# mLSTM stage: the old state's part is multiplied from unscaled q, scaled and added in SBUF, and the products that spread maxima and decays move behind the next turning and the k projection

## The reference

```python
mt = jnp.maximum(a, jnp.max(dmat, axis=-1))          # stabiliser of each token
w_inter = jnp.exp(a - mt)                            # weight of the old state
s = einsum('td,sd->ts', qb, kb) * jnp.exp(dmat - mt[..., None])
num = einsum('ts,sv->tv', s, vb) + w_inter[..., None] * einsum('td,dv->tv', qb, c)
den = jnp.sum(s, axis=-1) + w_inter * einsum('td,d->t', qb, n)
h = num / jnp.maximum(jnp.abs(den), jnp.exp(-mt))[..., None]
c_new = w_c * c + einsum('s,sd,sv->dv', w_s, kb, vb)
h_m = sigmoid(o) * rmsnorm(h, g_head)
```

## Time and profile before

| | |
|---|---|
| median of 3 runs | 2672.49 us (2671.37 to 2673.51) |
| the profiled execution: its time, its span | 2674.39 us, 2672.5 us |
| PE busy | 2589.0 us, 97% of the span |
| DVE busy | 1879.7 us, 70% |
| ACT busy | 906.3 us, 34% |
| chain that ended last | PE 88%, DVE 7% |
| mean granted clock of PE | 0.988 of full speed |

### The profile page before, as it was taken

One profiled execution on the slowest core, in us unless ns is written; L12 is line 12 of the kernel. 1 busy time (PEld: TensorE's weight loads), 2 busy tenths in 40 slices (PEclk: granted clock), 3 DMA queues, 4 the chain that ended last, 5 costly groups with the idle time before them and its releaser, 6 DMA issues.

```text
span 2672.5 us, 41483 instructions
## 1 busy us (share of the span) xinstructions
PE 2589.0 (97%) x14465; PEld 2239.6 (84%) x14465; DVE 1879.7 (70%) x3250; ACT 906.3 (34%) x2075; POOL 80.3 (3%) x167
## 2 busy tenths in 40 slices
PE   7999999999999998999999899999899999999998
PEld 6888888877887867999999798999778888887886
DVE  7666676764545568777777888888887887885444
ACT  4333333443333343222222333232432232342332
POOL 0000000000000000000000000000000000001010
PEclk9999999999999998999999999999999999999999
DMA  5112111442322334221111441222242222234221
GB/s 205 56 56 82 55 55 62 162 151 95 106 106 91 109 108 163 88 67 63 63 63 63 150 134 63 94 67 90 63 152 79 78 64 77 78 138 173 89 71 54
DMA packets 165561, 252.72 MB, mean 95 GB/s; under 512 B 11168, under 2 KB 114696, under 8 KB 165480
## 3 DMA queue, kind: packets, MB, share of 16 engines
q1 hardware_dynamic: 163128, 243.12, 27.4%
q0 software_dynamic: 2352, 8.52, 1.0%
HBM read 194.48 MB, written 56.95 MB: 94 GB/s over the span
## 4 chain that ended last, share of the span: by engine, by line
PE 88%; DVE 7%; issue 2%; ACT 1%; DMA 1%; POOL 0%; SPq 0%; DVEq 0%; ACTq 0%; POOLq 0%
PE m_proj L112 12%; PE m_proj L114 12%; PE m_proj L113 12%; PE m_turned L112 6%; PE m_turned L113 6%; PE m_turned L114 6%; PE m_acc L114 5%; PE m_acc L113 5%; PE m_acc L112 5%; PE m_pair L112 4%; PE m_pair L113 4%; PE m_pair L114 4%; PE m_pair L1222 1%; DVE f_acc L2142 1%; PE m_turned L1230 1%
## 5 line engine op out<-in xcount | busy, mean ns | idle before, releaser
L1916 ACT ACTIVATE f_up_hi<-f_sums 128x512 fp32r<-128x512 f32 x144 | 89.5, 622 | 544.1 <-DVE f_sums L2098 497.0
L2114 DVE TENSOR_TENSOR f_part<-f_part,m_acc 128x384 f32<-128x384 f32 (+2 forms) x240 | 119.3, 514 | 144.3 <-PE m_acc L114 142.0
L112 PE MATMUL m_proj<-f_down_hi,f_uT_hi 128*128 128x512 f32 x512 | 205.0, 400 | 8.1 <-DVE f_acc L2142 7.9
L112 PE MATMUL m_turned<-f_down_hi,f_uT_hi 128*128 128x512 f32 x512 | 201.4, 393 | 10.5 <-DVE f_down_lo L2111 10.5
L113 PE MATMUL m_turned<-f_down_lo,f_uT_hi 128*128 128x512 f32 x512 | 201.3, 393 | 0.0
L114 PE MATMUL m_turned<-f_down_hi,f_uT_lo 128*128 128x512 f32 x512 | 201.0, 393 | 0.0
L113 PE MATMUL m_proj<-f_down_lo,f_uT_hi 128*128 128x512 f32 x512 | 200.6, 392 | 0.0
L114 PE MATMUL m_proj<-f_down_hi,f_uT_lo 128*128 128x512 f32 x512 | 200.6, 392 | 0.0
L2142 DVE TENSOR_TENSOR f_acc<-f_acc,m_turned 128x1024 f32<-128x1024 f32 x143 | 166.3, 1163 | 34.3 <-PE m_turned L114 32.2
L2142 DVE TENSOR_TENSOR f_acc<-f_acc,m_proj 128x1024 f32<-128x1024 f32 x128 | 156.1, 1219 | 46.5 <-PE m_proj L114 46.5
L1932 ACT ACTIVATE f_uT_hi<-f_part 128x256 fp32r<-128x256 f32 (+1 forms) x320 | 98.3, 364 | 206.7 <-PE m_turned L114 124.8
(11 more groups left out here) (389 smaller groups left out, 7146.6 us busy)
## 6 DMA issues: line engine op xcount, KB each, us to landing
f_up_raw<-in_w_up SPq DMA_DIRECT2D x96, 512.0 KB, 5.3
f_down_raw<-in_w_down SPq DMA_DIRECT2D x96, 512.0 KB, 5.3
hT_hi_kept<-m_hT_hi SPq DMA_DIRECT2D x17, 512.0 KB, 4.9
hT_lo_kept<-m_hT_lo SPq DMA_DIRECT2D x17, 512.0 KB, 5.7
a_hT_hi<-hT_hi_kept SPq DMA_DIRECT2D x17, 512.0 KB, 3.6
a_hT_lo<-hT_lo_kept SPq DMA_DIRECT2D x17, 512.0 KB, 4.6
m_x<-in_x_prompt SPq DMA_DIRECT2D x16, 512.0 KB, 4.2
a_x_sum<-in_x_prompt SPq DMA_DIRECT2D x16, 512.0 KB, 6.4
```

What stands on the lines that cost most here:

```text
L112: eng.matmul(out, lh(k), rh(k), start=f, stop=False)
L1916: act.activation(up_hi[:, q], weight(q), ACT.Copy).then_inc(up_hi_made, 1)
L2114: dve.tensor_tensor(part[out][:, 0:w], part[other][:, 0:w], up_ps[bank][:, 0:w], ALU.add).then_inc(combined, 1)
```

## The change

It does five things.

1. q is no longer scaled (DVE L796) and no scaled q is turned (PE L672) or copied (ACT L549).
2. The old state's part is multiplied from unscaled turned q right behind the v projection, four products into `past`, a view of `turned`. DVE scales it out of PSUM with the column of w_inter into a new SBUF tile `num`.
3. `acc` holds the tokens' part alone; DVE adds it to `num` in SBUF ahead of the final part. The final part, the four squares on ACT and `heads` then read `num`. The squares wait for the sum, and the wait for the squares moves three small operations later.
4. On PE the products L637 to L641 move behind `turn_h` of the next tile and the k projection. On DVE the copies of COLS and the masking move behind `split_h` and `output_gate`; on ACT taking k moves ahead of the exponentials.
5. Waits: `turn_h` and the attention's first turning wait for `past_sb` in place of `qsT_sb`; the product into `acc` waits for `num_sb` of the tile before in place of the end of `heads`.

```diff
 # scalar(act), body
             if exists(r + 1):
                 split_h(tile_at(r + 1, 1 - slot))
+            if exists(i) and not first_round(r):
+                take_k(cur)
...
-            if exists(i) and not first_round(r):
-                take_k(cur)
...
-            if exists(j):
-                all_of(act, qs_turned, j)
-                all_of(act, squared, j - 1)
-                act.activation(qsT[:, :, 0:mix.n], turned[:, 0:HEADS, 0:mix.n], ACT.Copy).then_inc(qsT_sb, 1)
...
-                all_of(act, num_ps, j)
+                all_of(act, num_sb, j)
                 reached(act, fin_step, (j - 1) * FIN_STEPS + 10)
                 for h in range(HEADS):
-                    ins = act.activation(junk[0:mix.n, h, :], acc[0:mix.n, h, 0:QK], ACT.Square, accum_out=fin[0:mix.n, 3, h:h + 1])
+                    ins = act.activation(junk[0:mix.n, h, :], num[0:mix.n, h, 0:QK], ACT.Square, accum_out=fin[0:mix.n, 3, h:h + 1])
 # tensor(pe), body
+            if exists(r + 1):
+                turn_h(tile_at(r + 1, 1 - slot))
+            if exists(i) and not first_round(r):
+                all_of(pe, o_sb, i - 1)
+                project(proj[1], cur, w_k, k_ps)
             if exists(j):
                 all_of(pe, row_act, j, ROW_ACTS)
...
-            if exists(r + 1):
-                turn_h(tile_at(r + 1, 1 - slot))
-            if exists(i) and not first_round(r):
-                all_of(pe, o_sb, i - 1)
-                project(proj[1], cur, w_k, k_ps)
...
-                all_of(pe, q_scaled, j)
                 all_of(pe, qT_sb, j)
                 all_of(pe, kT_sb, j)
+                if m == P:
+                    all_of(pe, C_moved, j - 1)
+                state = C if m == P else C_dec
                 for h in range(HEADS):
-                    ins = pe.transpose(turned[:, h, 0:m], q[0:m, mix.slot, h * QK:(h + 1) * QK], ident[0:m, 0:m])
-                ins.then_inc(qs_turned, 1)
+                    ins = pe.matmul(past[0:m, h, :], qT[:, h, 0:m], state[:, h, :], start=True, stop=True)
+                ins.then_inc(past_ps, 1)
...
-                all_of(pe, fin_step, j - 1, FIN_STEPS)
+                all_of(pe, num_sb, j - 1)
...
                 for h in range(HEADS):
-                    pe.matmul(acc[0:m, h, 0:VA], qsT[:, h, 0:m], state[:, h, :], start=True, stop=False)
-                    ins = pe.matmul(acc[0:m, h, 0:VA], decay[0:m, h, 0:m], v[0:m, mix.slot, h, :], start=False, stop=True)
+                    ins = pe.matmul(acc[0:m, h, 0:VA], decay[0:m, h, 0:m], v[0:m, mix.slot, h, :], start=True, stop=True)
 # vector(dve), body
-            if exists(j):
-                all_of(dve, cols_ps, j)
...
             if exists(r + 1):
                 split_h(tile_at(r + 1, 1 - slot))
...
                 if exists(i):
                     output_gate(mix)
+                all_of(dve, cols_ps, j)
+                dve.tensor_copy(cols[0:m, 0:12], COLS[0:m, 0:12]).then_inc(cols_sb, 1)
+                dve.tensor_copy(cols[:, 12:16], COLS[:, 12:16]).then_inc(cols_sb, 1)
+
+                all_of(dve, num_ps, j - 1)
+                dve.scalar_tensor_tensor(decay[0:m, :, 0:m], wide[0:m, :, 0:m], -1.0,
...
-                qv = q[0:m, mix.slot, :].rearrange("p (h d) -> p h d", h=HEADS)
-                dve.tensor_tensor(qv, qv, cols[0:m, 4:8].unsqueeze(2).to_broadcast([m, HEADS, QK]), ALU.mult).then_inc(q_scaled, 1)
...
+                all_of(dve, past_ps, j)
+                all_of(dve, cols_sb, j, 2)
+                all_of(dve, fin_step, j - 1, FIN_STEPS)
+                dve.tensor_tensor(num[0:m], past[0:m], cols[0:m, 4:8].unsqueeze(2).to_broadcast([m, HEADS, VA]), ALU.mult).then_inc(past_sb, 1)
                 all_of(dve, scores_ps, j)
...
-                all_of(dve, squared, j)
-                dve.tensor_tensor(f(0), acc[0:m, :, QK], cols[0:m, 8:12], ALU.max).then_inc(fin_step, 1)
+                dve.tensor_tensor(num[0:m], num[0:m], acc[0:m, :, 0:VA], ALU.add).then_inc(num_sb, 1)
+                all_of(dve, num_sb, j)
+                dve.tensor_tensor(f(0), num[0:m, :, QK], cols[0:m, 8:12], ALU.max).then_inc(fin_step, 1)
...
                 dve.reciprocal(f(2), f(1)).then_inc(fin_step, 1)
                 dve.wait_ge(fin_step, base + 6)
+                all_of(dve, squared, j)
                 dve.tensor_tensor(f(4), f(3), f(2), ALU.mult).then_inc(fin_step, 1)
 # attention, tensor(pe)
-                pe.wait_ge(*m.qsT_sb)
+                pe.wait_ge(*m.past_sb)
```

More of the change, by code:

```diff
@@ L213 @@
     o_sb: object
-    qsT_sb: object
+    past_sb: object
     cols_sb: object
@@ L296, in mlstm_programs @@
     x, gmix = sb("x", [P, 2, D]), sb("gmix", [P, D])
+    hT_hi, hT_lo = sb("hT_hi", [P, 2, KC, P], F32R), sb("hT_lo", [P, 2, KC, P], F32R)
+    num_at = sb.next
     w_raw = sb("w_raw", [P, PC])
-    hT_hi, hT_lo = sb("hT_hi", [P, 2, KC, P], F32R), sb("hT_lo", [P, 2, KC, P], F32R)
+    num = Place(nc, "m_", num_at, IDENT_AREA)("num", [P, HEADS, VA])
     q, k = sb("q", [P, 2, MW]), sb("k", [P, 2, MW])
     v, o = sb("v", [P, 2, HEADS, VA]), sb("o", [P, 2, MW])
-    qkT, qsT = sb("qkT", [P, 2, HEADS, P]), sb("qsT", [P, HEADS, P])
+    qkT, junk = sb("qkT", [P, 2, HEADS, P]), sb("junk", [P, HEADS, P])
     qT, kT = qkT[:, 0], qkT[:, 1]
@@ L356, in mlstm_programs @@
     proj = [both[:, 0, :], both[:, 1, :]]
-    turned = ps("turned", [P, KC, P])
+    turned = ps("turned", [P, KC, P])[:]
     pair = ps("pair", [P, 2, NB])
@@ L363, in mlstm_programs @@
     first_q, first_k = (acc[:, 2 * n:2 * n + 2, :].rearrange("p a b -> p (a b)") for n in (0, 1))
-    junk = qsT
+    past = turned.rearrange("p c t -> p (c t)").rearrange("p (h v) -> p h v", h=HEADS)[:, :, 0:VA]
     ident_made, consts_in, const_sb = sem("ident_made"), sem("consts_in"), sem("const_sb")
@@ L374, in mlstm_programs @@
     cols_ps, cols_sb, masked, decayed = (sem(n) for n in ("cols_ps", "cols_sb", "masked", "decayed"))
-    qk_turned, qT_sb, kT_sb, q_scaled, k_scaled = (sem(n) for n in ("qk_turned", "qT_sb", "kT_sb", "q_scaled", "k_scaled"))
-    qs_turned, qsT_sb, scores_ps, state_ps = (sem(n) for n in ("qs_turned", "qsT_sb", "scores_ps", "state_ps"))
+    qk_turned, qT_sb, kT_sb, k_scaled = (sem(n) for n in ("qk_turned", "qT_sb", "kT_sb", "k_scaled"))
+    past_ps, past_sb, num_sb, scores_ps, state_ps = (sem(n) for n in ("past_ps", "past_sb", "num_sb", "scores_ps", "state_ps"))
     weighted, C_made, C_moved, num_ps, squared, fin_step, out_done, state_out = (
@@ L738, in heads @@
                 at = slice(h * QK, (h + 1) * QK)
-                ins = dve.scalar_tensor_tensor(heads_out[0:m, at], acc[0:m, h, 0:QK], fin[0:m, 7, h:h + 1], o[0:m, t.slot, at],
+                ins = dve.scalar_tensor_tensor(heads_out[0:m, at], num[0:m, h, 0:QK], fin[0:m, 7, h:h + 1], o[0:m, t.slot, at],
                                                ALU.mult, ALU.mult)
@@ L773, in body @@
                 yield
+            if exists(r + 1):
+                split_h(tile_at(r + 1, 1 - slot))
             if exists(j):
+                if on_round(r, 1):
+                    dve.wait_ge(late_in, 16 * N_LATE)
+                if exists(i):
+                    output_gate(mix)
                 all_of(dve, cols_ps, j)
@@ L786, in body @@
             if exists(j):
-                if on_round(r, 1):
-                    dve.wait_ge(late_in, 16 * N_LATE)
-                if exists(i):
-                    output_gate(mix)
                 all_of(dve, qk_turned, j)
                 dve.tensor_copy(kT[:, :, 0:m], turned[:, HEADS:2 * HEADS, 0:m]).then_inc(kT_sb, 1)
-                all_of(dve, cols_sb, j, 2)
-                qv = q[0:m, mix.slot, :].rearrange("p (h d) -> p h d", h=HEADS)
-                dve.tensor_tensor(qv, qv, cols[0:m, 4:8].unsqueeze(2).to_broadcast([m, HEADS, QK]), ALU.mult).then_inc(q_scaled, 1)
                 if on_round(r, NT + 1):
@@ L858, in body @@
                 f = lambda a: fin[0:m, a, :]
-                all_of(dve, squared, j)
-                dve.tensor_tensor(f(0), acc[0:m, :, QK], cols[0:m, 8:12], ALU.max).then_inc(fin_step, 1)
+                dve.tensor_tensor(num[0:m], num[0:m], acc[0:m, :, 0:VA], ALU.add).then_inc(num_sb, 1)
+                all_of(dve, num_sb, j)
+                dve.tensor_tensor(f(0), num[0:m, :, QK], cols[0:m, 8:12], ALU.max).then_inc(fin_step, 1)
                 dve.wait_ge(fin_step, base + 4)
-                dve.scalar_tensor_tensor(f(1), acc[0:m, :, QK], -1.0, f(0), ALU.mult, ALU.max).then_inc(fin_step, 1)
+                dve.scalar_tensor_tensor(f(1), num[0:m, :, QK], -1.0, f(0), ALU.mult, ALU.max).then_inc(fin_step, 1)
                 dve.wait_ge(fin_step, base + 5)
@@ L877, in mlstm_programs @@
                     q_ps=(q_ps, NT + 1), k_ps=(k_ps, NT + 1), v_ps=(v_ps, NT + 1), o_ps=(o_ps, NT + 1), v_sb=(v_sb, NT + 1), o_sb=(o_sb, NT + 1),
-                    qsT_sb=(qsT_sb, NT + 1), cols_sb=(cols_sb, 2 * (NT + 1)), weighted=(weighted, NT + 1),
```

(1 more changed line is left out.)

11 lines of the change are left out of this document (3 added, 8 removed).

## The result

The median went from 2673.0 us (4 runs) to 2697.9 us (4 runs, 2697.2 to 2698.7): ratio 1.0091, 95% interval 1.0079 to 1.0103. The change makes the kernel slower by 0.9%. The direction was forecast; the size was not: 2687 with a range to 2697. The profiled execution of after took 2697.21 us with a span of 2695.4, that is 22.9 more than the span of before.

A forecast was written before the change was run, and what follows sets the result against it. PE was taken to bound the kernel, with a lengthened DVE and ACT chain newly holding it. Profiled 2674.4 + 11.8 (rounds) - 0.9 (other rounds) + 3.4 (hand-over) = 2688.7; less 1.9 for the median, 2686.8, given as 2687, range 2676 to 2697.

The forecast's parts named there:

- What bounds the kernel: In the thirteen mLSTM rounds: PE sets the pace, busy 381.00 of 381.35 us, 29.33 us a round.
- PE's own saving: On PE in each round: four transposes go, 0.44 us, and the stall at L637 goes, 0.19 us.
- that case: At turn_gates: PE is not held, so a round takes 28.73 us and the time is 2667; chance 8%.
- The chain to the copies, steps 1 to 7: From T0 (v projection's end) over DVE and ACT to L598: PE waits 1.5 us, round 30.24, +11.8 us over 13 intervals.
- step 4: ACT's squares start only after DVE's addition and take 1.27 us; L866 stands at T0 + 13.48, against 11.63.
- The other rounds, - 0.9: Rounds 1, 15 and 16: a similar wait in round 1, shorter chains in 15 and 16, together -0.9 us.
- the clock as a rival that holds in every round or in none: PE's clock falls after the stall in each of thirteen rounds: +22 us, 2709 in all; chance 4%.
- The price of one spell, 1.7: One spell of slow clock on PE costs 4 x 0.43 = 1.7 us.
- The lower of the two rows that I bounded the stall between: PE idle of 0.9 us between 44 and 45 left the clock at 1.00; the upper row was 2.04 us.
- the sum and squares of tile 16 come once more, ... 1.0: At the hand-over to attention: tile 16's sum and squares add 1.4 us, 0.4 of it covered, so 1.0.
- The hand-over's first part, 2.4: On DVE before attention: tile 15's sum and squares 1.4, tile 16's scaling of past 0.6, later start 0.4 us.
- The scaling of q that went: On DVE at the hand-over: its removal frees nothing, since it filled the time of POOL's power.

The follow-up runs named there:

- the first experiment: Kernel after, with DVE's copies of the columns and the masking of decay moved ahead of output_gate: 2673.05 us, ratio 1.0000 to the kernel before.
- only the order: Kernel before, with the change's reordering on PE, DVE and ACT, but q scaled, turned and added by PE as before: 2672.82 us, ratio 0.9998.
- the work in the gap: Kernel after, with six more products, their result overwritten, on PE ahead of the gates' turning in rounds 2 to 14: 2692.29 us, ratio 1.0070.
- the early addition: Kernel after, with DVE's addition of the past moved ahead of the norm of the tile two rounds on: 2679.26 us, ratio 1.0021.

## Why the prediction came out too low

*What bounds the kernel, and PE's own saving: right.* With PE free of the stall (the first experiment) a round is 28.86; the forecast for that case was 28.73. The four transposes give the 0.42 between 29.28 (only the order) and 28.86, against 0.44. Of the 0.19 of stall at L637, the order alone gave back 0.05.

*The chain to the copies, steps 1 to 7: right.* Each mark was within 0.25 us, and the stall's place and releaser were those named. It made 12.7 us in the rounds where the sum had 11.8 (13.1 with the two rounds that are longer for another reason than the clock). The 0.9 between 12.7 and 11.8 is 0.07 a round, most of it step 4: L865 came 0.23 later than summed, since the squares began 0.81 behind the addition (I had 0.72) and L865 0.11 behind their end, not 0.03; PE then followed the copies' end by 0.05, not 0.14, and took half of it back. The squares' own 298 ns a piece lie between the two rows that bounded them, 277 and 309.

*The other rounds, - 0.9: right* (- 0.15 at the first T0, - 0.74 over the last two rounds).

*The step that failed first: the clock as a rival that holds in every round or in none.* I gave 4% to thirteen spells and nothing to some. It fell in three of thirteen, 4.0 to 4.4 us in all, that is 1.3 to 1.5 us each. The price of one spell, 1.7, was nearly right. The lower of the two rows that I bounded the stall between was misread: the window from 44 to 45 cuts its idle time short. PE ended L599 at 44.11 and started again at 45.36:

```profile
45.36 0.36 PE L112 MATMUL m_pair<-m_og_hi,m_hT_hi 128*128 128x264 f32 x1 [1.24 <-DVE m_rows L809]
```

So 1.24 us had gone by without a fall, and 2.04 were followed by one; the stalls of 1.33 lay just above the lower bound, and some had a fall and some not. That called for a case of its own, a fall in some of the rounds, and the sum had no term for it. By the Trainium skill, "TensorE: Matmul & The Clock Gate", section "A second HAM failure mode: psum-queue depth-cycling", PE that idles for short moments between groups of matmuls often enough goes back and forth between its two rates; the trace agrees with that here, three times in thirteen rounds at 1.3 us.

*The step that failed second: "the sum and squares of tile 16 come once more, ... 1.0".* It was 3.4 in this trace (17.49 less 14.11), and 2.9 in that of the first experiment (16.96). I had priced the squares as a delay of DVE's finish, and not asked what ACT has behind them. Before, ACT's squares waited for PE alone and were done at 530.86, 1.05 us ahead of the attention's first turning:

```profile
529.76 0.27 ACT L570 ACTIVATE m_qsT<-m_acc 32x128 f32<-32x128 f32 x1 [4.80 <-PE m_acc L703]
...
530.68 0.18 ACT L570 ACTIVATION_READ_ACCUMULATOR m_qsT<-m_acc 32x1 f32 x1
```

Now they wait for an addition that stands behind the attention's constants on DVE, and ACT's copy of the rows and a_qT wait with them, and PE with these. DVE was not the bound there any more, though the sum had it so: its L1360 now waits 2.10 us for PE, where L1361 had waited 0.41. Moving the addition took 2.5 of the 3.4 away; the rest came together with a low clock over the first products, which was not tested by itself.

*The hand-over's first part, 2.4: right in size (2.6) and in its terms.* By distances between starts on DVE in after: up to `w_last` + 0.47 (forecast 0.4); from there to L865 + 1.50, that is 0.71 for tile 15's addition and 0.79 for the wait for its squares (1.4); tile 16's scaling of the past + 0.60 (0.6). The scaling of q that went gave nothing back, as forecast: a wait of 0.6 for POOL's power stands in its place.

The two misses, 4.4 (0.4 of it not the clock's) and 2.4, and the 0.9 of the chain make 7.7 of the 8.6 us between 14.3 and the 22.9 of the spans; the rest is 0.2 ahead of the first turning and 0.6 behind the hand-over. A further 2.6 us lies in the runs: I took off 1.9 because the profiled execution of before lay that much above its median, but that of after lay 0.7 below its own.

*Left open.* Why the clock fell at every fourth stall, at 184, 307 and 430 us, and not at the others of the same length, no run tells. In the two other traces with the same rounds it fell at 275 and 398 only, so the places are not fixed by the kernel. That idle time is its cause, the work in the gap shows; what picks the rounds was not tried. The low clock at the hand-over, too, falls in other places from trace to trace, and no run separates its part from that of the order.

## What to carry to other kernels

When a change puts an operation of one engine between two that were independent (here an addition on DVE between PE and ACT's squares), list what the second engine has queued behind it at every place, the one odd tile at a change of stage above all; that is where 2.9 to 3.4 us came from against a forecast of 1.0. When PE must stand idle for a short time in every round, count a fall of the clock in some rounds as a case of its own: the full price was put at 22 us here, and the falls cost 4.0 to 4.4; with stalls of 2.5 us they cost 1.7 a round on average, of the 3.0 of a full one. And look for the instruction that holds a small buffer: moving two copies of 0.16 us, and a masking of 0.68 with them, ahead of a gate of 4.4 us was worth 24.9 us, as much as the whole change had cost.

## What the runs showed of the hardware

The clock's answer to the same idle time was not the same each time. Stalls of 0.35 us on average in thirteen rounds (the early addition): no fall. Stalls of 1.33 us in a round of 30.3: half clock for some 3 us behind the stall, in every fourth round in the trace of after, and in two of thirteen rounds in two other traces of the same rounds; a stall of 1.60 us passed without one. Stalls of 2.5 us in a round of 31.4: a loss of 3.0 in each of the first three rounds, then of 0, 1.6 and 3.0 us in turn. Filling the 1.33 us with products that nobody reads kept the clock at 1.00 over all thirteen rounds and made the kernel faster by 5.6 us than the same one without them.
